# The first output tile's products interleaved with the last five row tiles' normalization in a hybrid decoder step

## The chip, the cores and the metric

One NeuronCore of one Trainium2 chip. The metric is the device time of one launch in microseconds. Engines: PE (TensorE), DVE (VectorE), ACT (ScalarE), POOL (GpSimd) and SP (SyncE, which here only issues DMAs).

## The reference

One layer of a decoder trunk, for a prompt of 1024 rows and 8 sample rows of 2048 values each, 1032 rows together, in float32:

```
h = rmsnorm(x, g_mix); z = h @ w_in             (2048 x 5632)
mixer A: three dilated windows, 16 heads x 64;  mixer B: window 128, 16 query heads on 4 kv heads
branches * silu(gates) -> concat -> w_out -> residual add
x = x + (p @ w_ple) * sigmoid(rmsnorm(x, g_ple) @ w_pg);  y = rmsnorm(x, g_final)
```

The change touches the first line alone.

## The kernel before, in words

**Products.** Every float32 matrix is kept as two parts, `hi` (rounded to the PE's fp32r) and `lo` (what is left over), and each product is three matmuls (`three`, L855 to L857): w_hi by x_hi, w_hi by x_lo, w_lo by x_hi. The input stands transposed in SBUF, `act_hi` and `act_lo` with 16 blocks k of 128 input columns, by 1032 rows. An output tile is 128 columns of z. It is computed in three units u of 344 rows each (t = 0, 1, 2), each a chain of 16 x 3 = 48 matmuls into one PSUM bank, `u % 2`. So the first tile is units 0, 1 and 2: rows 0 to 343, 344 to 687 and 688 to 1031. From unit 2 on a unit waits until its bank's last user has been copied out by ACT (`bank_free`). Everything beside the products (attention and the rest) is put between them by a table of positions 16 * u + k (`EVENTS`), of which none lies before position 16.

**Opening.** The 1032 rows come in nine row tiles i of 128 rows (the last has the 8 sample rows). For each, in this order:

- SP loads `x_in` (two buffers; the load of tile i waits until tile i - 2 is normalized);
- ACT squares and sums it (L1020, into `x_n`, and so only when PE has transposed tile i - 2 out of that buffer), DVE finishes the mean (L1256), ACT takes the root (L1022), DVE inverts it (L1241 to L1244) and writes `x_n` (L1259);
- PE transposes `x_n` in four quarters q of four blocks (L645); quarter number 4i + q goes to one of eight PSUM banks in turn;
- ACT copies each quarter to `act_hi` (L1015), then DVE subtracts to get `act_lo` (L1251), which sets `x_lo`.

ACT and DVE run one tile behind with these last two: tile i - 1 is split after tile i was squared (ACT) and normalized (DVE). Only when all 36 quarters are in `act_lo` does PE begin with unit 0:

```
            pe.wait_ge(sem("x_lo"), 4 * len(ROW_TILES))
            for u in range(ZPAIR):
```

**Weights.** Weight group g is four k blocks of one tile's weights (256 KB). SP loads it to `w_raw` (two buffers, so group g waits for the split of group g - 2), POOL rounds it (L629) and subtracts (L631) into a ring of five slots. Groups 0 to 3 are the first tile, group 4 begins the second; group 5 takes group 0's slot when unit 2 has used it. SP issues groups 0 and 1 after the second row tile's load and groups 2 to 6 after the last row tile's.

Of the kernel before, what the change touches and what calls it, by code (L numbers as in the profile page):

```python
# [9 lines left out]
ACT = mybir.ActivationFunctionType  # L10
AX = mybir.AxisListType

P = 128
# [27 lines left out]

ZS = {**{ZQA + j: j for j in range(8)}, **{ZKA + j: 8 + j for j in range(8)}, **{ZVA + j: 16 + j for j in range(8)},
      **{ZQB + j: 24 + j for j in range(8)}, ZKB: 32, ZKB + 1: 33, ZVB: 34, ZVB + 1: 35}


CHUNKS = [(b, k0, min(512, (b + 1) * BLK - k0)) for b in range(QB) for k0 in range(0, (b + 1) * BLK, 512)]
# [137 lines left out]
def build(nc, a, o):  # L184
# [25 lines left out]
    with ctx:  # L210
# [85 lines left out]
        def _(sp):  # L296
# [19 lines left out]
            for i, (r0, n) in enumerate(ROW_TILES):  # L316
                if i >= 2:
                    sp.wait_ge(sem("x_normed"), i - 1)
                sp.dma_start(x_in[0:n, i % 2, :], x_p[r0:r0 + n, :] if i < 8 else x_s).then_inc(sem(f"x_loaded{i % 2}"), 16)
                if i == 1:  # L320
                    weights(0)
                    weights(1)
            for g in range(2, 7):
                weights(g)

            def load_zq(kind, n, half):
# [307 lines left out]
        def _(pe):  # L634

            pe.wait_ge(sem("consts"), 48)
            for i, (r0, n) in enumerate(ROW_TILES):
                pe.wait_ge(sem("x_normed"), i + 1)
                for q in range(4):
                    u = 4 * i + q  # L640
                    if u >= 8:
                        pe.wait_ge(sem("x_lo"), u - 7)
                    for m in range(4):
                        k = 4 * q + m
                        mm = pe.transpose(psum[:, u % 8, n * m:n * m + n], x_n[0:n, i % 2, k * P:(k + 1) * P], ident[0:n, 0:n])  # L645
                    mm.then_inc(sem("x_turned"), 1)

            def a_step(n_, s_):
# [211 lines left out]
                if k % WG == 0:  # L860
                    pe.wait_ge(sem("w_split"), GROUP[what, tile, k] + 1)

            pe.wait_ge(sem("x_lo"), 4 * len(ROW_TILES))
            for u in range(ZPAIR):
                tile, t = divmod(u, 3)
                for k in range(KT):
                    for e in EVENTS.get(16 * u + k, ()):
                        beside(e)
                    if t == 0:
                        group_wait("in", tile, k)  # L870
                    if k == 0 and u >= 2:
                        pe.wait_ge(sem("bank_free"), u - 1)
                    mm = three(u % 2, "in", tile, k, t, k == KT - 1)
                    if k == KT - 1:
                        mm.then_inc(sem("produced"), 1)
                    elif t == 2 and k % WG == WG - 1:
                        mm.then_inc(sem("w_used"), 1)
# [130 lines left out]
        def _(act):  # L1008

            def x_hi_copies(i):  # L1010
                r0, n = ROW_TILES[i]
                for q in range(4):
                    u = 4 * i + q
                    act.wait_ge(sem("x_turned"), u + 1)
                    act.activation(act_hi[:, 4 * q:4 * q + 4, r0:r0 + n], psum[:, u % 8, 0:4 * n].rearrange("p (m r) -> p m r", m=4), ACT.Copy).then_inc(sem("x_hi"), 1)  # L1015
            for i, (r0, n) in enumerate(ROW_TILES):
                act.wait_ge(sem(f"x_loaded{i % 2}"), 16 * (i // 2 + 1))
                if i >= 2:
# [211 lines left out]
        def _(dve):  # L1230
# [15 lines left out]
            def x_lo_parts(i):  # L1246
                r0, n = ROW_TILES[i]
                for q in range(4):
                    u = 4 * i + q
                    dve.wait_ge(sem("x_hi"), u + 1)  # L1250
                    dve.tensor_tensor(act_lo[:, 4 * q:4 * q + 4, r0:r0 + n], psum[:, u % 8, 0:4 * n].rearrange("p (m r) -> p m r", m=4),  # L1251
                                      hi32[:, 4 * q:4 * q + 4, r0:r0 + n], ALU.subtract).then_inc(sem("x_lo"), 1)
            dve.wait_ge(sem("consts"), 48)
            for i, (r0, n) in enumerate(ROW_TILES):
# [325 lines left out]
```

## Time and profile before

| | |
|---|---|
| median of 3 runs | 2594.65 us (2591.0 to 2595.0) |
| the profiled execution's own time | 2592.9 us |
| its span in the trace | 2591.1 us |
| PE busy | 2445.8 us, 94% |
| DVE, ACT, POOL busy | 32%, 24%, 26% |
| first product starts | 67.23 us |
| mean granted clock of PE | 0.974 |

The profile shows one execution. "Busy" of an engine is the time in which it has an instruction. In the timeline, each row has a start, a duration and in brackets the idle time before it and what ended it; consecutive products overlap a little, so the distance between two starts is what one costs. A granted clock of 1.00 is 2.4 GHz, 0.50 is 1.2 GHz.

### The profile page before, as it was taken

What the parts mean: (1) busy time and instruction counts of PE and PEld (TensorE: products, weight loads), DVE (VectorE), ACT (ScalarE), POOL (GpSimd) and SP (SyncE); (2) the same over time, 40 slices, a digit from 0 to 9 for tenths busy, and PEclk for the clock granted to TensorE, in tenths of its full rate; (3) what the DMA queues carried; (4) which work ended last, traced back from release to release, by engine and by line L of the source; (5) the groups of instructions that cost most, each with busy time, mean ns of one, the idle gap of its engine ahead of it and who ended that gap; (6) DMA issues with size and microseconds to landing.
All of it is one profiled execution on the core that took longest, in us unless ns stands there. A gap on an engine that the chain in (4) does not pass through costs nothing.

```text
span 2591.1 us, 40760 instructions
## 1 busy us (share of the span) xinstructions
PE 2445.8 (94%) x16617; PEld 2284.7 (88%) x16617; DVE 816.9 (32%) x2172; ACT 611.4 (24%) x1462; POOL 676.7 (26%) x708
## 2 busy tenths in 40 slices
PE   3999999999999999999989999999999999999980
PEld 3998888888888999888878899999999999999980
DVE  7013323323223323445545434321110341111114
ACT  5012222222222212333545401210000221010013
POOL 2232222222222223112222223333233424233320
PEclk8999999999999999999999999999999999999995
DMA  5133223223223214444444453632322523223226
GB/s 173 56 106 104 83 84 104 82 86 106 86 86 101 76 58 144 120 128 139 140 122 150 120 168 110 198 92 80 98 91 78 180 76 89 86 81 93 78 85 257
DMA packets 315245, 284.82 MB, mean 110 GB/s; under 512 B 21170, under 2 KB 283498, under 8 KB 311706
## 3 DMA queue, kind: packets, MB, share of 16 engines
q1 hardware_dynamic: 278226, 237.96, 30.3%
q10 hardware_dynamic: 36832, 44.25, 4.8%
q8 instruction: 132, 2.16, 0.4%
q14 instruction: 55, 0.44, 0.1%
HBM read 213.38 MB, written 68.76 MB: 109 GB/s over the span
## 4 chain that ended last, share of the span: by engine, by line
PE 87%; DVE 6%; DMA 4%; ACT 2%; issue 1%; SPq 1%; POOL 0%; ACTq 0%; DVEq 0%; POOLq 0%
PE psum L855 24%; PE psum L857 23%; PE psum L856 23%; PE psum L660 3%; PE psum L676 3%; PE psum L688 3%; PE psum L716 1%; PE psum L900 1%; DMA s_ring<-in_cache_a_k 1%; PE psum L731 1%; PE psum L744 1%; DMA out<-f_out 1%; DVE x_n L1259 1%; DVE act_lo L1251 1%; DVE s_prod L1352 1%
## 5 line engine op out<-in xcount | busy, mean ns | idle before, releaser
L855 PE MATMUL psum<-act_hi,w_hi 128*128 128x344 f32 x4032 | 1319.1, 327 | 11.9 <-DVE t_y L1544 4.5
L857 PE MATMUL psum<-act_hi,w_lo 128*128 128x344 f32 x4032 | 1292.2, 320 | 0.0
L856 PE MATMUL psum<-act_lo,w_hi 128*128 128x344 f32 x4032 | 1291.6, 320 | 0.0
L855 PEld LDWEIGHTS psum<-act_hi,w_hi 128*128 128x128 f32 x4032 | 763.0, 189 | 22.0 <-issue 10.9
L856 PEld LDWEIGHTS psum<-act_lo,w_hi 128*128 128x128 f32 x4032 | 762.4, 189 | 0.2
L857 PEld LDWEIGHTS psum<-act_hi,w_lo 128*128 128x128 f32 x4032 | 762.0, 189 | 0.0
L629 POOL CAST w_hi<-w_raw 128x512 fp32r<-128x512 f32 (+1 forms) x352 | 224.6, 638 | 1789.4 <-PE psum L857 1625.4
L631 POOL TENSOR_TENSOR w_lo<-w_raw,w_hi 128x512 fp32r<-128x512 f32 (+1 forms) x352 | 456.7, 1297 | 28.2
L1282 DVE COPY prob_t<-psum 128x512 f32<-128x512 f32 (+2 forms) x96 | 53.5, 558 | 470.3 <-PE psum L688 470.3
L1061 ACT ACTIVATE prob<-prob,mx 128x256 f32<-128x256 f32 (+7 forms) x128 | 98.4, 770 | 145.6 <-DVE mx L1310 145.6
L1055 ACT ACTIVATE prob_t<-psum 128x512 f32<-128x512 f32 (+2 forms) x96 | 47.1, 491 | 353.8 <-PE psum L688 353.8
L1304 DVE CUSTOM_DVE_ANT_0 prob<-psum,bias 128x512 f32<-128x512 f32 (+2 forms) x192 | 98.6, 551 | 96.0 <-PE psum L660 96.0
L1507 DVE TENSOR_TENSOR sq<-h_row 128x344 f32<-128x344 f32 x48 | 24.8, 517 | 301.4 <-ACT h_row L1174 300.3
L1540 DVE TENSOR_TENSOR t_gate<-psum,acc 128x344 f32<-128x344 f32 x48 | 24.8, 516 | 287.4 <-PE psum L857 287.4
L1213 ACT ACTIVATE t_gate<-t_gate 128x344 f32<-128x344 f32 x48 | 23.6, 491 | 355.9 <-DVE t_gate L1540 355.9
L676 PEld LDWEIGHTS psum<-prob_t,v_nat 128*64 128x64 f32 x1152 | 60.9, 136 | 51.4 <-issue 49.6
L1174 ACT ACTIVATE h_row<-psum 128x344 f32<-128x344 f32 x48 | 21.9, 457 | 324.0 <-PE psum L900 322.3
L1039 ACT ACTIVATE stage<-psum 128x344 f32<-128x344 f32 (+1 forms) x108 | 48.7, 451 | 186.5 <-PE psum L857 186.5
L660 PE MATMUL psum<-zk,zq 64*128 64x512 f32 (+3 forms) x384 | 88.0, 535 | 0.0
L676 PE MATMUL psum<-prob_t,v_nat 128*64 128x128 f32 x1152 | 84.1, 281 | 0.0
L688 PE MATMUL psum<-ident,prob 128*128 128x128 f32 x576 | 83.9, 282 | 0.0
L688 PEld LDWEIGHTS psum<-ident,prob 128*128 128x128 f32 x576 | 61.2, 140 | 17.0 <-issue 17.0
(180 smaller groups left out, 1753.6 us busy)
## 6 DMA issues: line engine op xcount, KB each, us to landing
w_raw<-in_w_in SPq DMA_DIRECT2D x208, 256.0 KB, 3.0
w_raw<-in_w_out SPq DMA_DIRECT2D x64, 256.0 KB, 2.8
w_raw<-in_w_pg SPq DMA_DIRECT2D x64, 256.0 KB, 2.8
z_scratch<-stage ACTq DMA_DIRECT2D x72, 172.0 KB, 1.8
h_scratch<-h_row ACTq DMA_DIRECT2D x16, 516.0 KB, 4.1
h_in<-h_scratch SPq DMA_DIRECT2D x48, 172.0 KB, 2.8
x_in<-in_x_prompt SPq DMA_DIRECT2D x8, 1024.0 KB, 5.0
zq<-z_scratch SPq DMA_DIRECT2D x32, 256.0 KB, 4.2
```

Of the source, the lines that this page charges most:

```text
L629: pool.tensor_copy(w_hi[:, slot, 0:n], w_raw[:, g % 2, 0:n]).then_inc(sem("w_rounded"), 1)
L631: pool.tensor_tensor(w_lo[:, slot, 0:n], w_raw[:, g % 2, 0:n], w_hi[:, slot, 0:n].bitcast(F32), ALU.subtract).then_inc(sem("w_split"), 1)
L660: pe.matmul(psum[:, 2 + h, 0:nk], zq[half, b * BLK:(b + 1) * BLK], zk[half, n_ % 2, k0:k0 + nk], start=True, stop=True).then_inc(sem("a_sc ...
L676: mm = pe.matmul(psum[HD * h:HD * h + HD, 6, (b % 4) * P:(b % 4 + 1) * P], v_nat[:, k0 // P + x, HD * h:HD * h + HD], prob_t[:, h, x * P:( ...
L688: mm = pe.transpose(psum[:, 4 + h, x * P:(x + 1) * P], prob_of(n, b)[:, h, k0 + x * P:k0 + (x + 1) * P], ident[:])
L855: pe.matmul(psum[:, bank, 0:T3], w_hi[:, slot, x, :], hi_a[:, k, rows], start=(k == 0), stop=False, skip_group_check=True)
L856: pe.matmul(psum[:, bank, 0:T3], w_hi[:, slot, x, :], lo_a[:, k, rows], start=False, stop=False, skip_group_check=True)
L857: return pe.matmul(psum[:, bank, 0:T3], w_lo[:, slot, x, :], hi_a[:, k, rows], start=False, stop=stop, skip_group_check=True)
L1039: act.activation(stage[:, slot, 0:w], psum[:, u % 2, 0:w], ACT.Copy).then_inc(sem("bank_free"), 1)
L1061: act.activation(pr, pr, ACT.Exp, bias=mx[:, b % 4, 4 + h:5 + h], accum_out=mx[:, b % 4, 6 + h:7 + h]).then_inc(sem("a_exped"), 1)
L1282: dve.tensor_copy(prob_t[:, 1, 0:nk], psum[:, 5, 0:nk]).then_inc(sem("a_copied1"), 1)
L1304: dve.tensor_tensor_reduce(prob_of(n, b)[:, h, k0:k0 + nk], psum[:, 2 + h, 0:nk], bias[:, h, u0:u0 + nk], SCALE, -3e38, ALU.add, ALU.max, ...
```

## The change

PE transposes only row tiles 0 to 3 at first. It then starts unit 0, and transposes row tiles 4, 5, 6, 7 and 8 just before positions 4, 8, 13, 19 and 27 (position 16 * u + k). Unit 0 waits for three divided row tiles, unit 1 for six, unit 2 for all nine. Since the products use banks 0 and 1, the quarters go round six banks (2 to 7) instead of eight, so quarter u waits for the dividing of quarter u - 6. SP issues weight group 2 after the load of row tile 2, group 3 after that of row tile 3 and group 4 after that of row tile 5.

```diff
@@ -41,6 +41,11 @@
 
 ZS = {**{ZQA + j: j for j in range(8)}, **{ZKA + j: 8 + j for j in range(8)}, **{ZVA + j: 16 + j for j in range(8)},
       **{ZQB + j: 24 + j for j in range(8)}, ZKB: 32, ZKB + 1: 33, ZVB: 34, ZVB + 1: 35}
+
+
+
+X_FIRST = 4
+X_LATER = {4: 4, 8: 5, 13: 6, 19: 7, 27: 8}
 
 
 CHUNKS = [(b, k0, min(512, (b + 1) * BLK - k0)) for b in range(QB) for k0 in range(0, (b + 1) * BLK, 512)]
@@ -317,10 +322,9 @@
                 if i >= 2:
                     sp.wait_ge(sem("x_normed"), i - 1)
                 sp.dma_start(x_in[0:n, i % 2, :], x_p[r0:r0 + n, :] if i < 8 else x_s).then_inc(sem(f"x_loaded{i % 2}"), 16)
-                if i == 1:
-                    weights(0)
-                    weights(1)
-            for g in range(2, 7):
+                for g in {1: (0, 1), 2: (2,), 3: (3,), 5: (4,)}.get(i, ()):
+                    weights(g)
+            for g in range(5, 7):
                 weights(g)
 
             def load_zq(kind, n, half):
@@ -634,15 +638,17 @@
         def _(pe):
 
             pe.wait_ge(sem("consts"), 48)
-            for i, (r0, n) in enumerate(ROW_TILES):
+
+            def x_turn(i):
+                r0, n = ROW_TILES[i]
                 pe.wait_ge(sem("x_normed"), i + 1)
                 for q in range(4):
                     u = 4 * i + q
-                    if u >= 8:
-                        pe.wait_ge(sem("x_lo"), u - 7)
+                    if u >= 6:
+                        pe.wait_ge(sem("x_lo"), u - 5)
                     for m in range(4):
                         k = 4 * q + m
-                        mm = pe.transpose(psum[:, u % 8, n * m:n * m + n], x_n[0:n, i % 2, k * P:(k + 1) * P], ident[0:n, 0:n])
+                        mm = pe.transpose(psum[:, 2 + u % 6, n * m:n * m + n], x_n[0:n, i % 2, k * P:(k + 1) * P], ident[0:n, 0:n])
                     mm.then_inc(sem("x_turned"), 1)
 
             def a_step(n_, s_):
@@ -860,12 +866,17 @@
                 if k % WG == 0:
                     pe.wait_ge(sem("w_split"), GROUP[what, tile, k] + 1)
 
-            pe.wait_ge(sem("x_lo"), 4 * len(ROW_TILES))
+            for i in range(X_FIRST):
+                x_turn(i)
             for u in range(ZPAIR):
                 tile, t = divmod(u, 3)
+                if u < 3:
+                    pe.wait_ge(sem("x_lo"), 4 * (3, 6, len(ROW_TILES))[u])
                 for k in range(KT):
                     for e in EVENTS.get(16 * u + k, ()):
                         beside(e)
+                    if 16 * u + k in X_LATER:
+                        x_turn(X_LATER[16 * u + k])
                     if t == 0:
                         group_wait("in", tile, k)
                     if k == 0 and u >= 2:
@@ -1012,7 +1023,7 @@
                 for q in range(4):
                     u = 4 * i + q
                     act.wait_ge(sem("x_turned"), u + 1)
-                    act.activation(act_hi[:, 4 * q:4 * q + 4, r0:r0 + n], psum[:, u % 8, 0:4 * n].rearrange("p (m r) -> p m r", m=4), ACT.Copy).then_inc(sem("x_hi"), 1)
+                    act.activation(act_hi[:, 4 * q:4 * q + 4, r0:r0 + n], psum[:, 2 + u % 6, 0:4 * n].rearrange("p (m r) -> p m r", m=4), ACT.Copy).then_inc(sem("x_hi"), 1)
             for i, (r0, n) in enumerate(ROW_TILES):
                 act.wait_ge(sem(f"x_loaded{i % 2}"), 16 * (i // 2 + 1))
                 if i >= 2:
@@ -1248,7 +1259,7 @@
                 for q in range(4):
                     u = 4 * i + q
                     dve.wait_ge(sem("x_hi"), u + 1)
-                    dve.tensor_tensor(act_lo[:, 4 * q:4 * q + 4, r0:r0 + n], psum[:, u % 8, 0:4 * n].rearrange("p (m r) -> p m r", m=4),
+                    dve.tensor_tensor(act_lo[:, 4 * q:4 * q + 4, r0:r0 + n], psum[:, 2 + u % 6, 0:4 * n].rearrange("p (m r) -> p m r", m=4),
                                       hi32[:, 4 * q:4 * q + 4, r0:r0 + n], ALU.subtract).then_inc(sem("x_lo"), 1)
             dve.wait_ge(sem("consts"), 48)
             for i, (r0, n) in enumerate(ROW_TILES):
```

PE's order before: the transposes of the eight full row tiles stand in one row, those of the ninth in the next, then come the products (names: `x_n` is the normalized row tile, `act_hi` and `act_lo` the transposed input).

```order
1 L645 MATMUL psum<-ident,x_n 128x128 x128
2 L645 MATMUL psum<-ident,x_n 128x8 x16
3 L855 MATMUL psum<-act_hi,w_hi 128x344
4 L856 MATMUL psum<-act_lo,w_hi 128x344
5 L857 MATMUL psum<-act_hi,w_lo 128x344
6 L855 MATMUL psum<-act_hi,w_hi 128x344
```

And now, from the start to the first interleaved row tile (lines 861 to 863 are 855 to 857 of before, 651 is 645):

```order
1 L651 MATMUL psum<-ident,x_n 128x128 x64
2 L861 MATMUL psum<-act_hi,w_hi 128x344
3 L862 MATMUL psum<-act_lo,w_hi 128x344
4 L863 MATMUL psum<-act_hi,w_lo 128x344
5 L861 MATMUL psum<-act_hi,w_hi 128x344
6 L862 MATMUL psum<-act_lo,w_hi 128x344
7 L863 MATMUL psum<-act_hi,w_lo 128x344
8 L861 MATMUL psum<-act_hi,w_hi 128x344
9 L862 MATMUL psum<-act_lo,w_hi 128x344
10 L863 MATMUL psum<-act_hi,w_lo 128x344
...
14 L651 MATMUL psum<-ident,x_n 128x128 x16
```

Twelve products now stand before the fifth row tile's transposes; the same pattern follows with 12, 15, 18 and 24 products between one row tile and the next. The last place is in unit 1:

```order
84 L861 MATMUL psum<-act_hi,w_hi 128x344
85 L862 MATMUL psum<-act_lo,w_hi 128x344
86 L863 MATMUL psum<-act_hi,w_lo 128x344
87 L651 MATMUL psum<-ident,x_n 128x8 x16
88 L861 MATMUL psum<-act_hi,w_hi 128x344
89 L862 MATMUL psum<-act_lo,w_hi 128x344
90 L863 MATMUL psum<-act_hi,w_lo 128x344
```

Behind the ninth row tile's transposes 15 products of the 96 of units 0 and 1 are left. On SP, before, and what its loads wait for:

```order
5 L319 DMA x_in<-in_x_prompt 128x2048 x2
6 L306 DMA w_raw<-in_w_in 128x4x128 x2
7 L319 DMA x_in<-in_x_prompt 128x2048 [waits x_normed] x6
8 L319 DMA x_in<-in_x_sample 8x2048 [waits x_normed]
9 L306 DMA w_raw<-in_w_in 128x4x128 [waits w_split] x17
```

and now:

```order
7 L324 DMA x_in<-in_x_prompt 128x2048 [waits x_normed]
8 L311 DMA w_raw<-in_w_in 128x4x128 [waits w_split]
9 L324 DMA x_in<-in_x_prompt 128x2048 [waits x_normed]
10 L311 DMA w_raw<-in_w_in 128x4x128 [waits w_split]
11 L324 DMA x_in<-in_x_prompt 128x2048 [waits x_normed] x2
12 L311 DMA w_raw<-in_w_in 128x4x128 [waits w_split]
13 L324 DMA x_in<-in_x_prompt 128x2048 [waits x_normed] x2
```

Three weight loads, each with a wait for POOL's splits, now stand ahead of later row tiles' loads in SP's queue.

## Rows read from the trace of the kernel before

**Rows 1.** Windows before, in and after the opening products.
```profile
core 0: us, PE busy (x) PEld busy (x) DVE busy (x) ACT busy (x) POOL busy (x), PEclk, DMA share, GB/s
15.00:67.00 52.00, 26.95 (x144) 24.01 (x144) 48.72 (x84) 33.17 (x60) 14.13 (x9) 0.73 0.42 143
67.20:85.30 18.10, 18.07 (x98) 18.07 (x99) 0.00 (x0) 0.46 (x1) 0.00 (x0) 0.83 0.08 25
85.30:2573.00 2487.70, 2400.75 (x16377) 2242.67 (x16376) 757.75 (x2066) 567.65 (x1390) 661.39 (x694) 0.98 0.35 109
```

**Rows 2.** Timeline of DVE, to 110 us: start, duration, form.
```profile
18.62 1.30 DVE L1242 SCALAR_TENSOR_TENSOR small<-small 128x1 f32<-128x1 f32 x1
...
34.48 2.48 DVE L1251 TENSOR_TENSOR act_lo<-psum,act_hi 128x512 fp32r<-128x512 f32 x4
...
38.12 2.35 DVE L1259 SCALAR_TENSOR_TENSOR x_n<-x_in,small,g_row 128x2048 f32<-128x2048 f32 x1
...
55.87 2.67 DVE L1259 SCALAR_TENSOR_TENSOR x_n<-x_in,small,g_row 128x2048 f32<-128x2048 f32 x1
58.47 2.47 DVE L1251 TENSOR_TENSOR act_lo<-psum,act_hi 128x512 fp32r<-128x512 f32 x4
...
62.05 2.34 DVE L1259 SCALAR_TENSOR_TENSOR x_n<-x_in,small,g_row 8x2048 f32<-8x2048 f32 x1
64.32 2.86 DVE L1251 TENSOR_TENSOR act_lo<-psum,act_hi 128x512 fp32r<-128x512 f32 x8
```

**Rows 3.** Timeline of PE, to 100 us: start, duration, idle before.
```profile
22.76 1.97 PE L645 MATMUL psum<-ident,x_n 128*128 128x128 f32 x16 [0.87 <-DVE x_n L1259]
28.70 3.57 PE L645 MATMUL psum<-ident,x_n 128*128 128x128 f32 x16 [3.97 <-DVE x_n L1259]
...
64.45 1.87 PE L645 MATMUL psum<-ident,x_n 8*128 8x8 f32 x16 [3.05 <-DVE x_n L1259]
...
67.68 0.49 PE L856 MATMUL psum<-act_lo,w_hi 128*128 128x344 f32 x1
67.97 0.49 PE L857 MATMUL psum<-act_hi,w_lo 128*128 128x344 f32 x1
...
73.34 0.32 PE L855 MATMUL psum<-act_hi,w_hi 128*128 128x344 f32 x1
73.50 0.32 PE L856 MATMUL psum<-act_lo,w_hi 128*128 128x344 f32 x1
```

**Rows 4.** Windows of the opening products, the two clock levels.
```profile
67.20:73.20 6.00, 5.97 (x21) 5.97 (x22) 0.00 (x0) 0.00 (x0) 0.00 (x0) 0.50 0.16 44
73.20:85.30 12.10, 12.10 (x79) 12.10 (x78) 0.00 (x0) 0.46 (x1) 0.00 (x0) 1.00 0.05 16
```

**Rows 5.** Timeline of ACT, 77.5 to 86 us: bank 1 is emptied.
```profile
85.33 0.46 ACT L1039 ACTIVATE stage<-psum 128x344 f32<-128x344 f32 x1 [7.00 <-PE psum L857]
```

**Rows 6.** Timeline of ACT, to 110 us: the ninth row tile's square.
```profile
56.81 1.89 ACT L1020 ACTIVATE x_n<-x_in 8x2048 f32<-8x2048 f32 x1
```

**Rows 7.** DMA issues to 53 us: KB each, median us to landing.
```profile
x_in<-in_x_prompt SPq DMA_DIRECT2D x8, 1024.0 KB, 5.0
...
w_raw<-in_w_in SPq DMA_DIRECT2D x3, 256.0 KB, 9.8
```

**Rows 8.** Timeline of POOL, to 130 us: weight splits.
```profile
15.88 2.67 POOL L629 CAST w_hi<-w_raw 128x512 fp32r<-128x512 f32 x1
18.64 1.27 POOL L631 TENSOR_TENSOR w_lo<-w_raw,w_hi 128x512 fp32r<-128x512 f32 x1
...
56.48 3.20 POOL L631 TENSOR_TENSOR w_lo<-w_raw,w_hi 128x512 fp32r<-128x512 f32 x1
```

**Rows 9.** Windows of 2 us on PE: busy, granted clock, DMA share, GB/s.
```profile
30.00:32.00 2.00, 2.00 (x11) 0.50 0.74 311
32.00:34.00 2.00, 0.27 (x2) 0.93 0.37 156
```

**Rows 10.** Waits of PE after 90 us, the longest: total, times, longest one.
```profile
PE psum L716 <- DVE mx L1339: 10.1, 4, 3.9
```

## The prediction

> **What bounds the kernel now.** I read the windows first. After the opening PE is busy for 2400.75 of 2487.70 us [rows 1]: it is the bound, and a microsecond by which it starts its products earlier should arrive at the end. In the opening, 15 to 67 us, it is the other way round: DVE is busy for 48.72 of 52 us, PE for 26.95 [rows 1]. Then, from 67.2 to 85.3 us, PE works alone through units 0 and 1, with DVE at 0.00 and ACT at 0.46 us. These 18.1 us need nothing that was missing at 67.2 except the last row tiles.
>
> DVE's timeline gives the pace. Each row tile costs a normalization (L1259) and four dividing operations (L1251), and the L1259 rows of tiles 4 and 7 start at 38.12 and 55.87: 5.92 us a tile [rows 2]. Row tile 2 is divided at 34.48 + 2.48 = 36.96; tile 8 is normalized at 62.05 + 2.34 = 64.39; the last quarter is divided at 64.32 + 2.86 = 67.18.
>
> PE's timeline gives the prices. A row tile's 16 transposes take 1.97 us at the full clock and 3.57 mostly at half; the ninth's take 1.87 at half. Products start 0.29 us apart at first (67.68, 67.97) and 0.16 later (73.34, 73.50) [rows 3]. The windows say why: the granted clock is 0.50 (1.2 GHz) until 73.2 and 1.00 (2.4 GHz) after it, with 21 products in the first 6.00 us [rows 4], 0.286 us each; the other 75 of the 96 take 12.1 us, 0.161 each.
>
> **The change, part by part.** *Products moved.* Unit 1 is complete when ACT starts to empty its bank, at 85.33 [rows 5]; unit 2 starts there. In the changed kernel 81 of the 96 products stand ahead of the ninth row tile's transposes. If PE keeps up, what follows 64.39 is these transposes (1.87 at most) and 15 products at 0.161, 2.4 us: unit 2 starts at 68.7. The dividing of the last quarter at 67.18 lies beside those products. ACT may empty unit 0's bank only after it, 67.18 + 0.46 = 67.6, also hidden.
>
> *Does PE keep up?* At the full clock: transposes 1.97 plus 12, 12, 15, 18 or 24 products at 0.161. For the gap after tile 4 that is 3.9 us, after tile 5 4.4, after tile 6 4.9, all below 5.92. After tile 7, normalized at 55.87 + 2.67 = 58.54, it is 1.97 + 3.86 = 5.8: done at 64.4, exactly when tile 8 is ready, with no slack. At half clock the four gaps cost 3.57 plus products at 0.286, so 7.0, 7.9, 8.7 and 10.4 us: PE falls behind in each. The clock therefore decides the last microsecond or two. Both levels will be granted: the average was 0.73 in 15 to 67 us with PE busy half the time [rows 1], and PE now has more to do. Behind 58.5 us each microsecond at half costs half a microsecond. I take a fifth of the ten, 1.1 us with what was carried over from before: unit 2 at 69.8. Ends: 68.2 (the ninth's transposes at the full clock) and 74, with half clock from tile 7 on: 58.54 + 10.4 + 1.9 = 70.9, and 15 products at 0.161 to 0.286 make 73.3 to 75.2.
>
> *Late transposes push back.* ACT's square of row tile i waits for the transposes of tile i - 2, and the ninth's starts at 56.81 [rows 6]. PE starts tile 6's transposes after 15 products, at the full clock in time. At half it is up to 2 us behind, ends them at about 59, and tile 8 is normalized 1 us late. This lies within the ends above.
>
> *Six banks instead of eight.* The fourth quarter waits for the second dividing operation of the tile before, 2 x 0.62 us after L1259 ends (2.48 for four); PE reaches it after 3 x 0.49 = 1.5 us. Cost 0.
>
> *Weight loads between row tiles.* Each is 256 KB behind a 1024 KB row tile on one queue. A row tile takes 5.0 us to land, and early weight loads took 9.8, since they stood behind others [rows 7]: the queue serves in order. Row tiles are requested one pace apart, 5.92 us, when the group ahead is nearly through. Cost 0; at the far end three times a quarter of a row tile's 5.0 us, 3.8 us, if each group delayed the row tile behind it and DVE felt all of it.
>
> *Splits of groups 2 to 4 move into the normalization.* The second group's rounding took 2.67 us and a later subtraction 3.20, where the others took 0.61 and 1.27 [rows 8]. DVE pays too: a 128x1 operation took 1.30 us beside POOL's subtraction at 18.64, and L1259 at 55.87 took 2.67 instead of 2.35 [rows 2]. The GPSIMD Engine Reference of the Trainium skill (section Specifications) says that POOL's SBUF interfaces are shared with VectorE, contended by instructions with two SBUF inputs; the trace agrees, L1259 having two. Three collisions cost between -0.3 (the 0.3 at 55.87 goes) and 3 x 1.3 = 3.9 us. I take 0, by where they fall: tile 3 is normalized at 38.12 - 5.92 + 2.35 = 34.6, and group 4 arrives some 5.6 us later, at 40.2; groups 3 and 2, behind tiles 1 and 0, two and nearly three paces sooner, at 28.3 and 23. All three fall near the start of L1251 (34.48 plus or minus whole paces), which reads PSUM and one SBUF tensor, and lasts longer than a split's 1.9 us.
>
> *Warm start of unit 2.* The 6.0 us at half clock after 67.2 are inside the 18.1, so they are not counted again.
>
> Sum: 85.3 - 69.8 = 15.5 us. The profiled execution took 2592.9 us, so 2577.4. The median is 1.75 us above that execution; I write 2578.
>
> **Rivals.** *PE's clock stays at half in the opening.* For it: 0.50 in most of those windows. Against it: with nothing but transposes in 30 to 32 us the next window had 0.93 [rows 9]. The Trainium skill's TensorE page (TensorE: Matmul & The Clock Gate, Part 4) says that transposes do not count as busy for the clock; by that rule the clock would stay down here. The trace disagrees. Time: from 36.96, 96 x 0.286 + 4 x 3.57 + 1.87 = 43.6 us, so 80.6. Before, the clock rose after 6.0 us of products, and the 24 between the last two turns last 6.9, so the ninth's transposes (some 1.0) and the last 15 products run at full: 77.8. Gain 7.5, time 2585.4.
>
> *DVE pays for POOL.* Three collisions at 1.3: gain 11.6, time 2581.3. For it: 1.30 and 2.67 [rows 2]. Against it: the arrival times above.
>
> *Given back later.* If something after the opening ran by its own time, PE would wait there. For it: only 87 us of PE idle time after 85.3 [rows 1]. Against it: these waits are on DVE's work that PE itself released, the longest 3.9 us [rows 10]. Time 2590 or more, within 0.2%.
>
> *Slower than before.* SP is in order: row tile 6's load stands behind group 4's, which waits for the split of group 2. Should DVE keep POOL out until it runs dry (tile 4 divided at 36.96 + 2 x 5.92 = 48.8), then split (1.9), load (5.0), square (1.9) and the root's steps (5.92 less DVE's two large rows, 1.1) put tile 6's L1259 at 58.7 instead of 38.12 + 2 x 5.92 = 50.0: 8.7 us. Unit 0 waits for group 3 as well. It decides when that happens twice, 17.4 against 15.5, with 6 us at half clock again (3 us): 2598. Against it: the longest hold seen was 3.20 instead of 1.27 [rows 8].
>
> **How the numbers follow.** Forecast 0.76, clock at half 0.08, POOL's collisions 0.09, given back 0.04, slower 0.03. A measurement of this kernel tells 0.2%, 5 us, from no change. The first three cases are faster by more: 0.93; same 0.04; slower 0.03. The range: the forecast with unit 2 at 68.2 is 2575.8, less 2 us of scatter between runs (2591.0 to 2595.0), 2573.5; on top, unit 2 at 73.3 or collisions, 2581.3, plus 2, 2583.5. Clock at half, given back and slower (0.15) stay outside.
>
> **What would show it.** First product at about 37 us; the ninth's transposes with x16 at 64.4 to 66; ACT's second copy out of a product bank (L1039 before) at about 69.8 instead of 85.33; DVE's pace still 5.92; POOL's third split near 24 us; PE busy time after unit 1 unchanged. It would be wrong if DVE's pace exceeded 6.3, or if PE were still in unit 0 at 64.

## The result and the profile after

The changed kernel takes 2577.67 us (median of 6 runs, 2575.82 to 2582.51), the kernel before beside it 2594.82 us (6 runs, 2591.0 to 2599.4). The ratio is 0.9939, with a 95% interval of 0.9925 to 0.9953. The profiled execution took 2577.41 us, 15.5 us less than that of before. Page of the changed kernel, span and busy times:

```profile
span 2575.6 us, 40761 instructions
...
PE 2440.8 (95%) x16617; PEld 2280.3 (89%) x16617; DVE 817.3 (32%) x2172; ACT 611.4 (24%) x1462; POOL 672.1 (26%) x708
```

Windows of the changed kernel: the same 52 us of the opening as in [rows 1], and 2487.70 us that end 18.1 us before the span's end, as the last row there does (columns as in rows 1):

```profile
15.00:67.00 52.00, 39.03 (x232) 36.63 (x233) 48.67 (x86) 33.30 (x60) 10.64 (x9) 0.87 0.44 148
...
69.80:2557.50 2487.70, 2399.01 (x16369) 2240.87 (x16367) 758.39 (x2066) 567.10 (x1389) 660.50 (x694) 0.98 0.35 109
```

In the opening PE is now busy for 39.03 us instead of 26.95 and the granted clock averages 0.87 instead of 0.73 (both averages hold some 14 us at the start in which the column can't be trusted; see the last section). DVE's 48.67 us are those of before (48.72). In the long window PE is busy for 2399.01 us, before for 2400.75; taken from the start of unit 2 itself, 68.50 to 2556.20, it is 2400.31. Behind the opening PE's busy time is that of before.

PE's timeline, against [rows 3]: the transposes of row tiles 3 to 8, and the first product (L861) before and after which they stand.

```profile
34.84 3.68 PE L651 MATMUL psum<-ident,x_n 128*128 128x128 f32 x16 [3.15 <-DVE x_n L1270]
38.17 0.64 PE L861 MATMUL psum<-act_hi,w_hi 128*128 128x344 f32 x1
...
41.05 1.91 PE L651 MATMUL psum<-ident,x_n 128*128 128x128 f32 x16
...
46.67 3.39 PE L651 MATMUL psum<-ident,x_n 128*128 128x128 f32 x16 [1.82 <-DVE x_n L1270]
...
52.58 1.97 PE L651 MATMUL psum<-ident,x_n 128*128 128x128 f32 x16
...
58.50 1.97 PE L651 MATMUL psum<-ident,x_n 128*128 128x128 f32 x16 [1.12 <-DVE x_n L1270]
...
64.34 1.01 PE L651 MATMUL psum<-ident,x_n 8*128 8x8 f32 x12
65.53 0.41 PE L651 MATMUL psum<-ident,x_n 8*128 8x8 f32 x4 [0.18 <-DVE act_lo L1262]
65.88 0.42 PE L861 MATMUL psum<-act_hi,w_hi 128*128 128x344 f32 x1
```

The first product starts at 38.17 us instead of 67.23. In brackets is PE's idle time: 1.82 us before row tile 5, 1.12 before row tile 7, none listed before 4, 6 and 8. PE reaches the ninth row tile's transposes at 64.34, when it is just normalized, and starts the last 15 products at 65.88. The 0.18 us before its last quarter is the only wait that six banks brought (for DVE's L1262).

The granted clock in windows of 2 us, the column behind PE's busy time, as in [rows 9]:

```profile
38.00:40.00 2.00, 2.00 (x9) 0.50 0.91 328
40.00:42.00 2.00, 2.00 (x16) 0.95 0.23 33
...
48.00:50.00 2.00, 2.00 (x11) 0.50 0.83 340
...
58.00:60.00 2.00, 1.50 (x14) 1.00 0.00 0
60.00:62.00 2.00, 2.00 (x16) 1.00 0.00 0
...
64.00:66.00 2.00, 1.73 (x19) 1.00 0.04 8
```

It is 0.50 from 30 to 40 us, then 1.00 except from 47 to some 50.4 us, and 1.00 from 51 us on. Before, the first 21 products ran at 0.50 [rows 4]; here the first six of unit 0 still do, but they no longer delay the end of unit 1, and the 15 behind the last row tile run at 1.00.

ACT's copies out of the two product banks, against [rows 5]. Unit 0's, unit 1's and unit 2's:

```profile
67.15 0.46 ACT L1050 ACTIVATE stage<-psum 128x344 f32<-128x344 f32 x1 [0.97 <-DVE act_lo L1262]
...
68.53 0.46 ACT L1050 ACTIVATE stage<-psum 128x344 f32<-128x344 f32 x1 [0.93 <-PE psum L863]
...
76.20 0.45 ACT L1050 ACTIVATE stage<-psum 128x336 f32<-128x336 f32 x1
```

Unit 1 ends at 68.53 instead of 85.33, 16.8 us sooner. Unit 0's copy waits for the last dividing operation and is ready long before unit 1 is.

DVE's timeline, against [rows 2]: normalization (L1270) of row tiles 4, 7 and 8, and the last dividing operations (L1262).

```profile
38.35 2.35 DVE L1270 SCALAR_TENSOR_TENSOR x_n<-x_in,small,g_row 128x2048 f32<-128x2048 f32 x1
...
56.09 2.35 DVE L1270 SCALAR_TENSOR_TENSOR x_n<-x_in,small,g_row 128x2048 f32<-128x2048 f32 x1
...
61.94 2.34 DVE L1270 SCALAR_TENSOR_TENSOR x_n<-x_in,small,g_row 8x2048 f32<-8x2048 f32 x1
64.21 2.86 DVE L1262 TENSOR_TENSOR act_lo<-psum,act_hi 128x512 fp32r<-128x512 f32 x8
```

From 38.35 to 56.09 is three times 5.91: DVE's pace is unchanged. Its last operation ends at 67.07 instead of 67.18, and the row at 56.09 takes 2.35 us, where before it took 2.67 beside a split. POOL's three moved splits, against [rows 8]:

```profile
24.04 0.61 POOL L633 CAST w_hi<-w_raw 128x512 fp32r<-128x512 f32 x1 [3.98 <-DMA w_raw<-in_w_in]
...
28.75 0.61 POOL L633 CAST w_hi<-w_raw 128x512 fp32r<-128x512 f32 x1 [2.74 <-DMA w_raw<-in_w_in]
...
40.75 0.61 POOL L633 CAST w_hi<-w_raw 128x512 fp32r<-128x512 f32 x1 [10.03 <-DMA w_raw<-in_w_in]
```

All three take 0.61 us, so they met no large DVE operation.

### The profile page after: what moved, and what is told of

It reads as the page before. It is cut to its first block, busy times and chain, and to the rows that moved or that the text cites. A ratio compares the mean times of both kernels' runs of the same rounds, so it can differ in the third digit from the quotient of the medians.

```text
span 2575.6 us, 40761 instructions
## 1 busy us (share of the span) xinstructions
PE 2440.8 (95%) x16617; PEld 2280.3 (89%) x16617; DVE 817.3 (32%) x2172; ACT 611.4 (24%) x1462; POOL 672.1 (26%) x708
## 4 chain that ended last, share of the span: by engine, by line
PE 86%; DVE 6%; DMA 4%; ACT 2%; SPq 1%; issue 1%; POOL 0%; ACTq 0%; DVEq 0%; POOLq 0%
PE psum L861 24%; PE psum L863 23%; PE psum L862 23%; PE psum L666 3%; PE psum L682 3%; PE psum L694 3%; DMA s_ring<-in_cache_a_k 2%; PE psum L722 1%; PE psum L911 1%; PE psum L750 1%; PE psum L737 1%; DMA out<-f_out 1%; DVE x_n L1270 1%; DVE s_prod L1363 1%; DVE s_sc L1370 1%
## 5 line engine op out<-in xcount | busy, mean ns | idle before, releaser
L861 PE MATMUL psum<-act_hi,w_hi 128*128 128x344 f32 x4032 | 1318.8, 327 | 10.9 <-DVE t_y L1555 4.5
L861 PEld LDWEIGHTS psum<-act_hi,w_hi 128*128 128x128 f32 x4032 | 762.3, 189 | 21.3 <-issue 11.1
```

The costliest lines, as they stand in the source:

```text
L861: pe.matmul(psum[:, bank, 0:T3], w_hi[:, slot, x, :], hi_a[:, k, rows], start=(k == 0), stop=False, skip_group_check=True)
```

## The experiments

All runs were timed beside the kernel before on their own chip. "Unit 1" is the start of ACT's copy of unit 1; "rest" is the span less that (in e4 that copy stood behind another one, and unit 2 began a little ahead of it, at 67.16). The span is that of the one profiled execution. e1 to e4 ran on one chip, e5 to e8 on a second, e9 to e11 on a third, e12 on a fourth; medians are best compared within such a group, and across groups by the ratio. Executions also differ by up to 0.6 us in when the ninth row tile is normalized, and differences of unit 1 hold that.

| run | unit 1, us | span, us | rest, us | median, us | ratio to before (95%) |
|---|---|---|---|---|---|
| before | 85.33 | 2591.1 | 2505.8 | 2594.82 | 1 |
| changed | 68.53 | 2575.6 | 2507.1 | 2577.67 | 0.9939 (0.9925 to 0.9953) |
| e1, all but the interleaving | 84.28 | 2590.1 | 2505.8 | 2592.35 | 0.9997 (0.9989 to 1.0006) |
| e2, weights late | 78.63 | 2584.4 | 2505.8 | 2587.99 | 0.9975 (0.9965 to 0.9985) |
| e3, 48 products left | 74.91 | 2582.1 | 2507.2 | 2583.58 | 0.9957 (0.9941 to 0.9972) |
| e4, 3 products left | 67.45 | 2576.4 | 2509.0 | 2579.37 | 0.9946 (0.9932 to 0.9961) |
| e5, 9 products left | 68.04 | 2580.1 | 2512.1 | 2577.14 | 0.9931 (0.9917 to 0.9946) |
| e6, no refinement | 62.49 | 2577.9 | 2515.4 | 2573.70 | 0.9919 (0.9902 to 0.9936) |
| e7, weights ahead | 69.49 | 2585.3 | 2515.8 | 2577.93 | 0.9931 (0.9913 to 0.9949) |
| e8, changed again | 68.31 | 2571.3 | 2503.0 | 2573.07 | 0.9914 (0.9900 to 0.9928) |
| e9, e6 again | 62.30 | 2571.2 | 2508.9 | 2571.88 | 0.9908 (0.9894 to 0.9921) |
| e10, changed a third time | 68.30 | 2574.7 | 2506.4 | 2575.62 | 0.9921 (0.9909 to 0.9934) |
| e11, mean early | 67.67 | 2573.7 | 2506.0 | 2575.45 | 0.9921 (0.9907 to 0.9934) |
| e12, e11 and e6 together | 61.73 | 2566.8 | 2505.1 | 2570.22 | 0.9914 (0.9900 to 0.9927) |

### e1: everything but the interleaving

```diff
-X_FIRST = 4
-X_LATER = {4: 4, 8: 5, 13: 6, 19: 7, 27: 8}
+X_FIRST = 9
+X_LATER = {}
...
-                    pe.wait_ge(sem("x_lo"), 4 * (3, 6, len(ROW_TILES))[u])
+                    pe.wait_ge(sem("x_lo"), 4 * len(ROW_TILES))
```

> All nine row tiles are transposed and divided before unit 0, as before the change; the early weight loads and the six banks stay. Theory (the whole gain is the 81 products that run beside the normalization): unit 1 ends at 85.3 +-1 us, as before (85.33), and the time is that of the kernel before within 0.1%. Rival (early weight loads or splits away from 56 us give part of it): the last quarter is divided 1 us or more before 67.2 and the time is 1 us or more under before's. Rival (six banks cost): PE's transposes wait on the dividing line L1262 and DVE's pace of 5.92 us a row tile rises.

ACT's timeline of e1, the copy of unit 1:

```profile
84.28 0.46 ACT L1050 ACTIVATE stage<-psum 128x344 f32<-128x344 f32 x1 [7.00 <-PE psum L863]
```

It stands at 84.28 against 85.33 [rows 5], and the ratio's interval holds 1. The last dividing operation ends at 66.58 instead of 67.18: 0.26 us because this execution's row tile 0 was that much ahead, 0.32 because the collision at 55.87 [rows 2] is gone. The 96 products, up to the copy of unit 1, then took 17.7 us instead of 18.15. The early weights and six banks do not explain the gain; the interleaving does.

### e2: the weights as late as before

```diff
-                for g in {1: (0, 1), 2: (2,), 3: (3,), 5: (4,)}.get(i, ()):
+                for g in {1: (0, 1)}.get(i, ()):
                     weights(g)
-            for g in range(5, 7):
+            for g in range(2, 7):
                 weights(g)
```

> The interleaving stays, but weight groups 2 to 4 are loaded after the last row tile, as before the change. Theory (PE is in order, so a product that waits for its weights also holds the transposes behind it, and through them ACT and DVE): PE stands in unit 0 at block 8 until group 2 is split at about 58 us, the ninth row tile is normalized at about 69 instead of 64.3, unit 1 ends at about 75.5 instead of 68.5, so some 2585 us. Rival (weights do not matter, since POOL is idle anyway and units 0 and 1 have slack): 68.5 and the time of the changed kernel. Rival (the holds add up): unit 1 ends after 85.3 and nothing is gained.

PE's timeline, the product that needs group 2, and ACT's copy of unit 1:

```profile
59.49 0.65 PE L861 MATMUL psum<-act_hi,w_hi 128*128 128x344 f32 x1 [11.35 <-POOL w_lo L635]
...
78.63 0.46 ACT L1050 ACTIVATE stage<-psum 128x344 f32<-128x344 f32 x1 [1.59 <-PE psum L863]
```

PE stands idle for 11.35 us until 59.49, as expected, and the row tiles' transposes stand behind it. Three fifths of the opening's gain are lost: unit 1 ends at 78.63, 3 us later than I had worked out. Group 2 was split at 59.44 and not at 58, since POOL's subtraction took 3.18 us once more, as in [rows 8]; and the granted clock was 0.50 when PE went on, so that it averaged 0.81 from 58 to 78 us. The moved loads bring nothing alone (e1) and are needed: with them late 6.7 us are gained, with them early 16.8.

### e3: 48 products behind the last row tile

```diff
-X_LATER = {4: 4, 8: 5, 13: 6, 19: 7, 27: 8}
+X_LATER = {2: 4, 5: 5, 8: 6, 12: 7, 16: 8}
```

> The five row tiles are transposed before positions 2, 5, 8, 12 and 16, so 48 products instead of 15 are left behind the ninth. Theory (what is left behind the last row tile is what the opening still costs): unit 1 ends at 64.3 + 1.1 + 48 x 0.157 = 72.9 us instead of 68.5, so 4.4 us over the changed kernel, about 2582. Rival (the gain comes from an earlier start of the products, at 37 us, wherever the last ones stand): the time of the changed kernel. Rival (the warm clock is most of the gain): between the two.

ACT's timeline of e3, the copy of unit 1:

```profile
74.91 0.46 ACT L1050 ACTIVATE stage<-psum 128x344 f32<-128x344 f32 x1 [7.67 <-PE psum L863]
```

It waited 7.67 us for PE and starts at 74.91: 6.4 us after the changed kernel's, where 33 more products at 0.157 make 5.2. The rest is the clock: PE had idled 2.03 us before the ninth row tile, and was granted 0.63 and 0.52 in 66 to 68 and 68 to 70 us. By the ratios (0.9957 and 0.9939) the total is some 4.7 us over the changed kernel's first measurement; these two intervals overlap, those of e3 and of e8 or e10 do not. The first product starts at 36.87 us, not later than there, so the early start by itself is not the gain. What is left behind the last row tile is what the opening costs.

### e4: 3 products behind the last row tile

```diff
-X_LATER = {4: 4, 8: 5, 13: 6, 19: 7, 27: 8}
+X_LATER = {4: 4, 9: 5, 15: 6, 23: 7, 31: 8}
```

> The five row tiles are transposed before positions 4, 9, 15, 23 and 31, so 3 products are left behind the ninth. Theory (below some number left, the last dividing operation and ACT's copy out of unit 0's bank set the start of unit 2): unit 2 starts at 67.1 + 0.5 = 67.6 us instead of 68.5, a gain of 0.9 us, at the limit of what can be measured. Rival (PE falls behind at half clock in the gaps with 24 products): the ninth row tile's transposes start 1 to 4 us after 64.3, unit 1 ends at 66.5 to 69, no gain or a loss of up to 2 us.

PE's timeline from the last product of unit 1 to the first three of unit 2, and a window of 2 us behind them (busy, granted clock):

```profile
65.70 0.32 PE L863 MATMUL psum<-act_hi,w_lo 128*128 128x344 f32 x1
67.16 0.44 PE L861 MATMUL psum<-act_hi,w_hi 128*128 128x344 f32 x1 [1.14 <-ACT stage L1050]
67.39 0.49 PE L862 MATMUL psum<-act_lo,w_hi 128*128 128x344 f32 x1
67.68 0.49 PE L863 MATMUL psum<-act_hi,w_lo 128*128 128x344 f32 x1
...
68.00:70.00 2.00, 2.00 (x9) 0.50 0.44 161
```

PE kept up, against the rival. Unit 2 starts at 67.16 (the theory had 67.6), 1.2 us before its first product in the changed kernel, at 68.34; half of that is that this execution's ninth row tile was 0.6 us ahead. But PE waited 1.14 us for bank 0, and the next products are 0.29 us apart: the granted clock is 0.50 in 68 to 70 us. Twelve products cost 1.5 us more, and unit 2's copy stands at 76.66, behind the changed kernel's 76.20. From the end of the ninth row tile's normalization to that copy it is 13.0 us here and 11.9 there, 1.1 us worse. Neither side had foreseen that.

### e5: 9 products

```diff
-X_LATER = {4: 4, 8: 5, 13: 6, 19: 7, 27: 8}
+X_LATER = {4: 4, 9: 5, 15: 6, 22: 7, 29: 8}
```

> The five row tiles are transposed before positions 4, 9, 15, 22 and 29, so 9 products are left behind the ninth, instead of 15 (the changed kernel) or 3 (the run with 31). Theory (unit 2 starts at the later of: bank 0 emptied, about 67.1; products done, 65.6 + 9 x 0.157 = 67.0, and PE, never idle for long, keeps the full clock): unit 2 starts at about 67.2 and its copy comes 7.6 us later, 1.3 us before the changed kernel's. Rival (any wait at bank 0 costs the clock, as in the run with 31, where 12 products at half followed a wait of 1.14 us): the granted clock is 0.50 for some 3.4 us from about 67 and unit 2 ends no sooner than in the changed kernel. Total time: 2576.5 or 2578, hardly to be told apart.

Windows of 2 us, PE busy and granted clock:

```profile
62.00:64.00 2.00, 1.44 (x12) 1.00 0.00 0
64.00:66.00 2.00, 1.81 (x18) 0.90 0.00 0
66.00:68.00 2.00, 2.00 (x8) 0.50 0.04 13
```

PE did not wait for bank 0 at all, and the clock fell all the same, behind 0.56 us of idle time before the ninth row tile and its small transposes. Unit 2's copy is at 76.25, 12.5 us after the ninth row tile's normalization instead of 11.9. So both halves of my expectation fell: the full clock was not kept, and a wait at bank 0 is not needed for the fall. Moving the ninth row tile's transposes further back than 27 has gained nothing in e4 or e5. Nor does the total gain: 2577.14 us, where the changed kernel on the same chip took 2573.07 (e8).

### e6 and e9: the root's refinement left out in the opening

```diff
-                inverse_root(n, small[0:n, i:i + 1], small[0:n, 9 + i:10 + i], small[0:n, 18 + i:19 + i])
+                chain(dve.reciprocal(small[0:n, 18 + i:19 + i], small[0:n, 9 + i:10 + i]))
...
-X_LATER = {4: 4, 8: 5, 13: 6, 19: 7, 27: 8}
+X_LATER = {4: 4, 9: 5, 14: 6, 20: 7, 27: 8}
```

> DVE leaves out the refinement of the root in the opening (one multiply-add, one halving and one reciprocal per row tile, 0.6 us with their waits), and the transposes stand before positions 4, 9, 14, 20 and 27, still 15 products behind the ninth. Theory (after the change DVE's pace sets the opening): pace 5.92 becomes 5.3 us, the ninth row tile is normalized at about 59.4 instead of 64.3, unit 1 ends at about 63.8 instead of 68.5, time 4.7 us under the changed kernel, 2573. Rival (PE is the next bound, since its gaps at half clock cost 7 to 9 us): unit 1 ends at 66 or later. Rival (the row tiles' loads, 5.0 us to landing with two buffers, are the next bound): the pace stays above 5.6.

> The kernel of e6 again (DVE leaves out the refinement of the root in the opening), beside the changed kernel. In its first profile unit 2 started at 62.5 us, 5.8 us before the changed kernel's, but from there to the end the span took 2515.4 us where others took 2503 to 2508, and the median was 2573.7 beside 2573.1. Theory (that loss is scatter between 900 and 1700 us after the start of unit 2, where the granted clock dips to 0.95 around waits, and not of the opening): over both sets of rounds this kernel is some 5.8 us faster than the changed one. Rival (what the opening gains beyond a point is given back there): no difference again.

DVE's normalizations of row tiles 6, 7 and 8 and ACT's copy of unit 1, in e6:

```profile
45.38 2.35 DVE L1270 SCALAR_TENSOR_TENSOR x_n<-x_in,small,g_row 128x2048 f32<-128x2048 f32 x1
...
50.66 2.35 DVE L1270 SCALAR_TENSOR_TENSOR x_n<-x_in,small,g_row 128x2048 f32<-128x2048 f32 x1
...
55.91 2.34 DVE L1270 SCALAR_TENSOR_TENSOR x_n<-x_in,small,g_row 8x2048 f32<-8x2048 f32 x1
...
62.49 0.46 ACT L1050 ACTIVATE stage<-psum 128x344 f32<-128x344 f32 x1 [0.92 <-PE psum L863]
```

The pace is 5.28 us and unit 1 ends at 62.49, 6.0 us before the changed kernel's (3.8 of it by the pace of the last six row tiles, 2.2 because row tile 2 is normalized that much sooner). DVE's pace does set the opening, and neither PE nor the loads took over. That much of the theory stands. The total doesn't follow it: over the ten timed executions of e6 and e9 the mean is 2573.0 us, over the ten of e8 and e10 2573.9. The expected 5.8 us were not seen there; 0.9 us was, and by the scatter of these executions the difference lies between about -2 and 4 us. On the one chip e6 was no faster than e8, on the other e9 lay 3.7 us under e10.

### e7: weight loads ahead of the row tiles'

```diff
+                for g in {2: (2,), 3: (3,), 5: (4,)}.get(i, ()):
+                    weights(g)
                 sp.dma_start(x_in[0:n, i % 2, :], x_p[r0:r0 + n, :] if i < 8 else x_s).then_inc(sem(f"x_loaded{i % 2}"), 16)
-                for g in {1: (0, 1), 2: (2,), 3: (3,), 5: (4,)}.get(i, ()):
+                for g in {1: (0, 1)}.get(i, ()):
                     weights(g)
```

> Weight groups 2, 3 and 4 are issued directly ahead of the loads of row tiles 2, 3 and 5 instead of behind them. Theory (one queue serves in order; 256 KB are 0.6 us at 420 GB/s): each of these row tiles lands 0.6 us later; only row tile 2's is felt, since ACT's square of it ends just when DVE is free, so the last dividing ends 0.5 us later and unit 2 starts at about 69. Rival (a weight load with its short pieces costs a quarter of a row tile's 5.0 us or more): 1.3 us or more each, unit 2 at 70 to 72. Rival (transfers are hidden anyway): 68.5. POOL's splits come at other times (about 23, 28 and 40), so a collision with L1270 or L1253 would add up to 1.3 us.

Timeline of e7: DVE at the mean of row tile 2, POOL's subtraction of a moved group, and DVE's normalization beside it.

```profile
25.68 0.15 DVE L1269 TENSOR_SCALAR small<-small 128x1 f32<-128x1 f32 x1 [0.84 <-ACT x_n L1033]
...
26.42 1.27 POOL L637 TENSOR_TENSOR w_lo<-w_raw,w_hi 128x512 fp32r<-128x512 f32 x1
...
26.94 2.90 DVE L1272 SCALAR_TENSOR_TENSOR x_n<-x_in,small,g_row 128x2048 f32<-128x2048 f32 x1
```

DVE waits 0.84 us for ACT's square, which began 0.8 us later behind row tile 1's normalization than in the changed kernel (3.55 us instead of 2.74), and the normalization takes 2.90 instead of 2.35 beside POOL's subtraction. From row tile 1's normalization to row tile 2's it took 6.85 us (20.09 to 26.94), in the changed kernel 6.04 (20.49 to 26.53). Together that is 0.81 + 0.55 = 1.36 us, and unit 1 ends 0.96 us after the changed kernel's though this execution's row tile 1 was 0.4 us ahead. Both costs that I had set at 0 for the change are real here; the order of the loads keeps them near 0. Who pays for such a meeting differs: here POOL's subtraction had begun first, at 26.42. Group 4's, at 39.58, met a normalization that had begun at 39.31, and there DVE kept its 2.35 us and POOL took 3.24 instead of 1.27. The median, 2577.93 us, is 4.9 over that of the changed kernel on the same chip (e8), and all four executions lie above all five of e8, though the intervals of the two ratios overlap. That is more than the opening lost. Where the rest of it comes from is not shown; the next section shows in which stretch the profiled execution lost it.

### e8 and e10: the changed kernel again

> The changed kernel again, beside the others. From the start of unit 2 to the end of the span it took 2507.1 us in its first profile and 2505.8 in the kernel before and in two variants of this study whose unit 2 starts at 84.3 and 78.6. Theory (the 1.3 us given back are scatter of the waits on DVE in the sample rows' attention, between 1200 and 1500 us): this time between 2505.5 and 2507.5, anywhere. Rival (an earlier unit 2 always loses about 1.3 us later): 2507 again. Unit 2 starts within 1.5 us of 68.5, by the clock that is granted in the opening.

> The changed kernel a third time, as the other half of the comparison. Theory: between 2573 and 2578 us, 0.6 to 0.8% under before. The remainder from unit 2's start to the end of the span lies between 2503 and 2513 us, and is long where the clock between 900 and 1700 us behind that start is low.

I had expected e8's rest between 2505.5 and 2507.5 us, or again 2507; it was 2503.0, outside both. e10's, 2506.4, lies within its range. Windows of PE, 1200 to 1400 us behind the start of unit 2, in e8:

```profile
core 0: us, PE busy (x), PEclk, DMA share, GB/s
1268.30:1468.30 200.00, 190.66 (x1360) 0.99 0.44 130
```

and in e7, whose rest was 12.8 us longer:

```profile
1269.50:1469.50 200.00, 186.15 (x1276) 0.95 0.41 123
```

In these 200 us e7 gets through 84 matmuls fewer (x1276, x1360); at 0.157 us each, a product's price, that is an estimated 13 us, about the whole difference. PE is busy for 4.5 us less in e7 and its granted clock is 0.95 instead of 0.99, around the waits for DVE in the sample rows' attention (the largest is PE's wait for DVE's mx: 16.1 us in all in e7, 11.9 in e8, 12.5 in the changed kernel's first profile, 10.1 in [rows 10]). The rest varies from 2503.0 to 2507.1 us in three profiles of one kernel, and from 2503.0 to 2515.8 over all. In the first 900 us behind the start of unit 2 PE is busy without a gap in every run.

### e11 and e12: the mean early, alone and with e6

```diff
                 for q in range(4):
                     u = 4 * i + q
+                    if q == 3 and i + 2 < len(ROW_TILES):
+                        x_mean(i + 2)
                     dve.wait_ge(sem("x_hi"), u + 1)
```

with the transposes before positions 4, 9, 14, 20 and 27. `x_mean` is the wait for the square and the operation that stood at the head of the next row tile.

> DVE finishes the mean of row tile i + 2 before the last dividing operation of tile i instead of behind it, so the root is there when DVE wants it; the arithmetic is that of the reference. The transposes stand before positions 4, 9, 14, 20 and 27. Theory (DVE's pace of 5.92 us holds 0.27 us of waiting for ACT's root): pace 5.65, the ninth row tile normalized at 62.4 instead of 64.3, unit 2 starts at 66.5, 1.9 us before the changed kernel's; below what the total time resolves. Rival (ACT or the loads then set the pace, since the mean waits for the square, which ends only 1 us before): the pace stays above 5.8 and DVE waits at the mean instead.

> The mean early (as in e11) and without the refinement of the root (as in e6 and e9): both steps that shorten DVE's pace. Where opening ends: pace 5.1 us, the ninth row tile normalized at about 58, unit 2 starts at about 62 or a little before, unless the row tiles' loads (5.0 us to landing and 5.1 us of square, root and normalization for every second tile) hold the pace at 5.2 or PE at half clock falls behind. What it tells apart: the opening of e6 and e9 was 6.0 us shorter than the changed kernel's, their mean time over ten executions only 0.9 us (2573.0 against 2573.9). If that is scatter, this kernel comes to 6 to 8 us under the changed kernel, 2567 to 2569; if what the opening gains is given back behind it, to 2572 to 2574.

In e11 row tiles follow each other after 5.55 us (48.80 and 54.35 in DVE's timeline), and the ninth is normalized at 62.2: what was expected, and a little more. But unit 1 ends at 67.67 instead of 66.5. Windows of e11, PE busy and granted clock:

```profile
64.00:66.00 2.00, 2.00 (x11) 0.70 0.00 0
66.00:68.00 2.00, 2.00 (x8) 0.50 0.24 88
```

The clock was at half behind the ninth row tile once more. In e12, with a pace of 5.03 to 5.09 us, it was 1.00 there and unit 1 ended at 61.73. The median is 2570.22 us, between the 2567 to 2569 of the one theory and the 2572 to 2574 of the other, so it does not decide between them. It is the lowest median of all, but on its chip the kernel before took less too (2593.81): the ratio is 0.9914, as that of e8. A gain over the changed kernel is not shown. It leaves the refinement out. The version with the reference's arithmetic, e11, cannot be told from the changed kernel (2575.45 beside 2575.62 on one chip).

## Why the prediction was right, and where not

**The sum.** Unit 2 was forecast at 69.8 us and started at 68.5; the gain of the opening was 16.8 us instead of 15.5. The term that was mis-sized is the clock behind 58.5 us: I charged 1.1 us for a fifth of ten microseconds at half, and the granted clock was 1.00 throughout. With 0 there my sum gives 68.7. e8 and e10 (68.31, 68.30) say the same. The last step of the sum does not add up as written: 2577.4 and 1.75 make 2579.2, not the 2578 that I wrote, and the lower end of the range, 2575.8 less 2, is 2573.8, not 2573.5.

**Products moved.** 81 of 96 beside the normalization, 15 behind it: shown by e3 (more left, more cost) and e1 (none moved, no gain). Of the 16.8 us some 2.6 are the clock and not the number of products: before, the first 21 took 0.286 us each where 0.161 is the price at the full clock.

**Does PE keep up.** At full clock I had the ninth row tile reached at 64.4 with no slack; it was 64.34. The first product came at 38.17, not about 37, since row tile 3's transposes ran at half clock (3.68 us; in e8 they took 2.72 and it came at 36.99). That cost nothing, since PE stood idle again before row tile 5.

**Late transposes, six banks, loads, splits.** All set at 0. ACT and DVE kept their pace, the quarters waited 0.18 us once, no row tile was late by more than 0.1 us (row tile 2, 6.04 us behind row tile 1, before 5.94), and the splits met L1262 and not L1270, at 24.0, 28.8 and 40.8 (I had 23, 28.3 and 40.2). e7 shows what they cost where they do not fall so well, 1.36 us for one of three, load and split together.

**From the opening to the end.** The profiled execution lost 1.3 us of the 16.8 behind the start of unit 2, which made its span's gain 15.5, just the number of the forecast. That agreement is partly luck: e8's rest was 2.8 us shorter than before's and its span is 2571.3. The three medians of the changed kernel, 2577.67, 2573.07 and 2575.62, lie 17, 22 and 20 us under before's. My 2578 is at their upper edge, and e8's 2573.07 lies just under the range. The opening accounts for 17 us; the up to 5 us beyond it in e8 and e10 are not explained and are of the size of the scatter.

**The rivals.** Half clock through the opening: excluded by the windows, where after transposes and a few products the level rose at 40 us. POOL's collisions: not here, e7 shows the mechanism. The slower case by SP's order did not occur: POOL's splits of 0.61 us show that DVE held none up. "Given back later" did not take the 12 us or more that it would have needed for 2590. Whether it takes a part of what the shorter openings gain further is open: e6, e9 and e12 start unit 2 some 6 to 7 us sooner than the changed kernel, but their ratios average 0.9914 and those of its three measurements 0.9925, some 3 us. Their rests were 2515.4, 2508.9 and 2505.1 us. I could not separate a slow stretch that follows from the earlier start from one that comes by chance.

## What to carry to other kernels

Where one engine prepares input at a fixed pace and another then works alone, count what must be left behind the last prepared piece, not how early the first work can start: 15 products instead of 96 was the gain, and 48 instead of 15 cost 6.4 us with as early a start. What the early work needs (here three weight loads) must be moved with it, behind the loads that set the pace and not ahead of them. With some 2500 us of later program that scatters by several microseconds, an edit of one or two microseconds is read from its own stage in the timeline, counted from the same event in both, not from the total.

## What the runs showed of the hardware that I had not expected

PE's granted clock fell to half close behind the ninth row tile's small transposes in e3, e4, e5 and e11, and not in the three profiles of the changed kernel or in e2, e6, e7, e9 and e12. PE's busy time there does not divide the two groups: in the window of 2 us that holds most of these transposes it is 1.79 to 1.81 us in e3, e4, e5 and also in e6, and 1.73 in the changed kernel's first profile (only e11's is lower, 1.59). What PE did directly beside them does. PE's timeline, e11 (it fell) and e8 (it did not):

```profile
62.25 1.01 PE L651 MATMUL psum<-ident,x_n 8*128 8x8 f32 x12 [0.22 <-DVE x_n L1277]
...
64.09 1.01 PE L651 MATMUL psum<-ident,x_n 8*128 8x8 f32 x12
```

Where it fell, PE had waited directly before these transposes (2.03 us in e3, 0.56 in e5, 0.22 in e11) or behind them (1.14 us, e4). In the eight profiles in which it did not fall, PE came from the products with at most 0.1 us between and went straight on to products, but for at most 0.19 us before the last quarter. That is a pattern in twelve profiles and not an explanation. Waits before the transposes of a full row tile were followed by a fall in one execution and not in another: 1.82 us before row tile 5 in the changed kernel's first profile, and half clock from 47 us; 2.05 us in the same place in e8, and 1.00.

What it costs is plain. In e4 12 products took 0.29 instead of 0.16 us, 1.5 us. From the end of the ninth row tile's normalization to unit 2's copy it is 11.9 us in the changed kernel's three profiles, in e6, e7, e9 and e12, and 13.5 us in e11, which leaves as many products behind it.

The same transposes ran at either price in different executions of one kernel: row tile 1's 16 took 1.97 us in e8 (and in before) and 3.67 in the changed kernel's first profile. The first row tile's took 3.65 in windows in which the column of the granted clock says 1.00, so that column is not to be trusted before its first change.

The Trainium skill's TensorE page (TensorE: Matmul & The Clock Gate, Part 4) says that transposes do not count as busy for the clock. In [rows 9] the level rose behind nothing but transposes; so it did in e1, where the first product comes at 66.63 us and the column reads 0.50 to 60 us and 1.00 in 62 to 64. In the changed kernel the opening had 1.00 from 51 us on with some 30% of PE's time up to 64 us in transposes; these float32 transposes did not keep it down. The measurement decides.
